# Issuing the V gather of a turn ahead of the U gather, in a hybrid mLSTM / attention / PEER encoder step

## What is computed

```
q = (xb @ w_q).reshape(TB, PEER_HEADS, PEER_KEY_DIM)
...
idx = jnp.take_along_axis(cidx, sel, axis=-1)
g = jax.nn.softmax(top.astype(jnp.float32), axis=-1).astype(xb.dtype)
u = jnp.take(expert_u, idx, axis=0)
a = jax.nn.gelu(jnp.einsum('thkd,td->thk', u, xb), approximate=False)
ve = jnp.take(expert_v, idx, axis=0)
return jnp.einsum('thk,thkd->td', g * a, ve)
```

## Time and profile before

| | before |
|---|---|
| median of 3 runs | 3383.86 us (3382.38 to 3389.47) |
| the profiled execution, its time | 3354.33 us |
| its span | 3352.6 us |
| VectorE busy | 2147.1 us (64%) |
| TensorE matmul busy | 2349.4 us (70%) |
| GpSimd busy | 1992.9 us (59%) |
| moved by DMA | 1197.59 MB, mean 357 GB/s |

### The profile page before, as it was taken

One profiled execution on the slowest core, in us unless ns is written; L12 is line 12 of the kernel. 1 busy time (PEld: TensorE's weight loads), 2 busy tenths in 40 slices (PEclk: granted clock), 3 DMA queues, 4 the chain that ended last, 5 costly groups with the idle time before them and its releaser, 6 DMA issues.

```text
span 3352.6 us, 42363 instructions
## 1 busy us (share of the span) xinstructions
PE 2349.4 (70%) x15147; PEld 1174.5 (35%) x15147; DVE 2147.1 (64%) x5579; ACT 535.9 (16%) x1059; POOL 1992.9 (59%) x2128
## 2 busy tenths in 40 slices
PE   8995775667667888877857765668567765675545
PEld 4652352335233533334534432325223431221111
DVE  1257757776676656657577667676676676766653
ACT  2211111211121221112121111111111111210001
POOL 0036666666666566665666666666666666666665
PEclk9996796678566988987867776678676875566555
DMA  6479999999999999999999999999999999999998
GB/s 229 149 277 405 358 349 375 362 373 349 375 357 381 368 402 408 408 400 357 362 353 365 366 369 363 360 372 351 376 361 374 364 353 377 359 359 362 368 368 325
DMA packets 348955, 1197.59 MB, mean 357 GB/s; under 512 B 37760, under 2 KB 54408, under 8 KB 346952
## 3 DMA queue, kind: packets, MB, share of 16 engines
q0 software_dynamic: 304128, 1107.43, 87.8%
q1 hardware_dynamic: 44616, 87.45, 7.1%
HBM read 1180.69 MB, written 14.15 MB: 356 GB/s over the span
## 4 chain that ended last, share of the span: by engine, by line
PE 31%; issue 16%; POOL 14%; DVE 13%; DMA 10%; another core or an unknown queue 9%; DVEq 5%; ACT 1%; ACTq 0%; SPq 0%; POOLq 0%
PE mx L1574 9%; PE acc L1675 7%; POOL ring L597 7%; POOL ring L586 7%; DVE ring L1273 6%; DMA ring<-in_peer_v_dram,idx 4%; PE mx L1385 3%; DMA ring<-in_peer_u_dram,idx 3%; DVEq L1145 2%; PE acc L1361 2%; PE mx L1585 2%; PE mx L1556 1%; DMA weights<-in_w_in_dram 1%; PE h2p L1628 1%
## 5 line engine op out<-in xcount | busy, mean ns | idle before, releaser
L1273 DVE SCALAR_TENSOR_TENSOR ring<-ring,h2p 128x1024 f32<-128x1024 f32 x1056 | 1272.2, 1214 | 551.7 <-DMA ring<-in_peer_u_dram,idx 267.5
L1675 PE MATMUL acc<-ring,wk 128*32 128x256 f32 x8448 | 1030.7, 507 | 684.6 <-DMA ring<-in_peer_v_dram,idx 317.5
L597 POOL DMA_INDIRECT ring<-in_peer_v_dram,idx x1056 | 995.3, 942 | 790.6 <-remote 369.4
L586 POOL DMA_INDIRECT ring<-in_peer_u_dram,idx x1056 | 995.8, 943 | 554.7 <-issue 302.4
L1675 PEld LDWEIGHTS acc<-ring,wk 128*32 128x32 f32 x8448 | 316.5, 129 | 1316.5 <-issue 776.9
L1574 PE MATMUL mx<-reg,weights 128*128 128x128 f32 x1792 | 275.3, 309 | 42.4 <-issue 42.1
L1574 PEld LDWEIGHTS mx<-reg,weights 128*128 128x128 f32 x1792 | 245.8, 216 | 101.5 <-issue 101.1
L1556 PE MATMUL mx<-weights,reg 128*128 128x512 f32 (+1 forms) x256 | 138.6, 668 | 1.9 <-DVEq L1246 1.1
L1385 PE MATMUL mx<-weights 128*128 128x512 f32 (+1 forms) x288 | 132.4, 604 | 2.2 <-issue 1.4
L1628 PE MATMUL h2p<-ch,ident 32*32 32x512 f32 x528 | 104.4, 798 | 31.2 <-issue 20.2
L828 ACT ACTIVATE gl<-dots 128x16 f32<-128x16 f32 x66 | 14.2, 216 | 537.8 <-issue 368.5
(11 more groups left out here) (311 smaller groups left out, 2425.6 us busy)
## 6 DMA issues: line engine op xcount, KB each, us to landing
ring<-in_peer_u_dram,idx POOLq DMA_INDIRECT x1056
ring<-in_peer_v_dram,idx POOLq DMA_INDIRECT x1056
weights<-in_peer_w_q_dram SPq DMA_DIRECT2D x7, 2048.0 KB
weights<-in_w_in_dram SPq DMA_DIRECT2D x5, 2048.0 KB, 18.2
weights<-in_w_in_dram SPq DMA_DIRECT2D x10, 1024.0 KB
ring<-in_peer_w_q_dram SPq DMA_DIRECT2D x8, 1024.0 KB, 6.1
xt<-in_x_prompt_dram SPq DMA_DIRECT2D x8, 512.0 KB
ring<-in_w_out_dram SPq DMA_DIRECT2D x2, 2048.0 KB, 13.6
```

Of the source, the lines that this page charges most:

```text
L586: pool.indirect_dma_start(ring[:, U_AT[n % NU], :], None, u_d, bass.IndirectOffsetOnAxis(ap=idx[:, g % 4, k:k + 1], axis=0)).then_inc(u_in ...
L597: pool.indirect_dma_start(ring[:, V_AT[n % NV], :], None, v_d, bass.IndirectOffsetOnAxis(ap=idx[:, g % 4, k:k + 1], axis=0)).then_inc(v_in ...
L1273: V.scalar_tensor_tensor(ring[:, U_AT[n % NU], :], ring[:, U_AT[n % NU], :], 1.0, h2p[:, :], ALU.mult, ALU.mult, accum_out=dots[:, (g + 1) ...
L1675: last = T.matmul(sums[g // 2 % 2][j * SUB:(j + 1) * SUB, :], wk[:, n // FEW % 5, n % FEW, :], ring[:, V_AT[n % NV], j * QD:(j + 1) * QD], ...
```

## The change

In a turn, the V gather of index n = 16 g + k is issued first and the U gather of index n + 16 behind it.

```diff
@@ -601,9 +601,9 @@
                 gather_u(0, k)
             for g in range(GROUPS):
                 for k in range(TOPK):
+                    gather_v(g, k)
                     if g + 1 < GROUPS:
                         gather_u(g + 1, k)
-                    gather_v(g, k)
 
 
         @block.scalar
```

## The result

The changed kernel takes 3392.2 us, the median of 20 runs (3383.5 to 3398.1), against 3384.05 us before, also of 20 runs: the ratio is 1.0020, with a 95% interval of 1.0012 to 1.0028. That is **8 us slower, where I forecast 27**. The sign was right and the size was not: the time lies under the 3395 to 3440 us that I had given for the forecast by itself.

The account below looks back on a forecast made before the run. The prediction saw a ring of several engines, each a little late for the next, none the bound by itself. Median 3384 us plus 27 us for late U gathers at group ends gave 3411 us; own range 3395 to 3440, full range 3353 to 3470.

Parts of the forecast that it names:

- GpSimd is held at V, not at U, and a held V gather keeps back U: GpSimd's queue: 328 holds at V gathers, almost none at U; each U gather behind one leaves 2.48 us later.
- The start costs nothing: First gathers: V gather 0 leaves some 12 us earlier, but the first V product waits for its weights; costed at nothing.
- Where VectorE was already waiting for U, the whole 2.48 us is passed on: 66 groups x 17.5% x 2.48 = 29 us: VectorE's last dot of each group: a U row one turn late costs the full turn where VectorE already waited; 29 us.
- lateness in the middle of a group is made good: VectorE's dots inside a group: it catches up before the group's end, so a late turn there was charged nothing.
- The second estimate, 11 U landings in the chain: Chain that ended last: left 11 times to a U landing, 11 x 2.48 = 27 us, the figure taken.
- transfers are the bound: DMA transfers from HBM: some 358 GB/s per core binds, order of issue moves nothing; 3384 us, chance 0.20 including catching up.
- TensorE gains more than VectorE loses: TensorE's V products: earlier V gathers save up to 1.7 us at each of 18 landings; 3353 us, chance 0.26.

Follow-up runs that it names:

- 6 and 8 buffers: 6 U and 8 V buffers in place of 7 and 7: ratio 1.0234 in the old order, 1.0100 with the V gather first, against the kernel before.
- half the bytes: Gathers fetch 512 floats in place of 1024: old order 0.9969 and 0.9968, new order 0.9956 and 0.9944, against the kernel before.
- Dot 1: Kernel before, with two extra VectorE multiplications by 1.0 ahead of the second dot behind `h2p` in every 32 dots: ratio 1.0031, 10 us slower.
- dot 31: Kernel before, with two extra VectorE multiplications by 1.0 ahead of the last dot of every second group: ratio 1.0020, 7 us slower.
- leads of 13: Kernel before, with 13 U gathers ahead of the V gathers in place of 17, for every first group of a pair 1.0141, for every second 1.0218.
- lead of 18: 18 U gathers ahead of V gather 0 in place of 17: ratio 1.0088; with 17 kept for indices 0 to 9 of 32: 1.0039.

## Why the prediction was right in sign and wrong in size

- **GpSimd is held at V, not at U, and a held V gather keeps back U**: right as a description of the waits. In both profiles of the change, V holds and VectorE's waits for U rose and TensorE's waits for V fell. With 6 and 8 buffers, where the holds at U have grown from 69 to 278 us, the same swap is a gain. But the sign of the time was in part luck: with half the bytes the same shift of waits went with a kernel that was 9 us faster.
- **The start costs nothing**: right; the first V products keep their time.
- **"Where VectorE was already waiting for U, the whole 2.48 us is passed on: 66 groups x 17.5% x 2.48 = 29 us"**: this is the step that failed, the term of the sum that was too large (27 us taken, 4 to 8 measured). The whole of a late turn is not passed on. Lateness put in by itself passed on 7 of 52 us ahead of a pair's last dot and 4 of 52 ahead of the other group's, a tenth of it in all. By the profiles of the two orders the rest is taken back from VectorE's waits for TensorE (`h2p`) and ScalarE (gelu), which mostly end when they did. The share was wrong as well, the other way: counted through the timeline, VectorE waited for U at 24 of the 66 last dots, 36% and not 17.5%, because its waits gather in the last four dots of a group (96 of 185). By the prediction's own rule that is 24 x 2.48 = 60 us, so the two errors partly cancelled. A tenth of 60 us is 6 us, which would fit the measured cost, but that is an estimate and no run shows that the cost is made up so.
- **"lateness in the middle of a group is made good"**, so charge only a group's end: wrong as a distinction. Dot 1 passes on a fifth, dot 31 an eighth. Delays of this size are mostly absorbed wherever they arise; leads of 13, which make one group in two late by four turns, cost 48 and 74 us.
- **The second estimate, 11 U landings in the chain**: it agreed with the first and was no confirmation. A second execution of the same kernel has 15 U and 15 V landings in its chain, where the first had 11 and 18, and the changed kernel has 18 and 16 in one execution and 16 and 18 in another. The count of landings in one chain therefore didn't price the change; that the pieces of several chains are nearly level here is my reading of it.
- **The rival "transfers are the bound"**: its time, 3384, was nearer than mine, but the half-byte kernels refute it as the bound of the whole: without half the gathered bytes the time falls by 0.3%. The part of it that named absorption was what happened, and that the order's cost vanishes with half the bytes says that the transfers bear on that cost. The rule in the Trainium skill, "DMA: Bandwidth & Descriptors", section Bandwidth, that for transfers between HBM and SBUF the HBM side binds at some 358 GB/s per core, doesn't set the time of this kernel: slices of it reach 402 to 411 GB/s, and at a mean of 191 GB/s in place of 357 it takes the same time within 0.3%.
- **TensorE gains more than VectorE loses**: not with 7 and 7 buffers, where TensorE gained 9 to 31 us in waits for V and VectorE lost 81 to 114 in waits for U. It did happen with 6 and 8 (55 gained, 34 lost).

What stays open: which resource fixes the level time of the ring. It is not the bytes and not VectorE's wait for U. What makes up the 4 to 8 us that the order does cost, and why they turn into a gain with half the bytes, is open too. Stops of GpSimd of 369 us are put down to `remote`, and no run took them apart. Why a lead of 18 still costs 13 us once more than half of the added holds at U are avoided isn't settled either.

## What to carry to other kernels

An in-order queue that feeds two rings makes the second stream wait whenever the first is held. Find out at which of the two it is held, from the waits of the issuing engine: the gather behind the held one is the one that comes late. Whether that costs time only a timed run says: here the same swap of order gave +0.2%, -1.3% with another split of the buffers, and -0.3% with half the bytes. And before the full length of a new wait is charged, look at how long the same engine waits right behind it for somebody else; a wait that grows in front of another wait mostly just moves, as long as the other is long enough, and the surest price is a run that inserts a known delay at that place.

## What was not expected of the hardware

A DMA busy share of nine tenths did not mean that the transfers were the limit. With half the bytes the gathers' queue still shows 57.0% of the 16 engines' time in place of 87.8%, not half of it. And the same kernel took 3384 us on one chip and 3360 on another, 0.7% apart, more than three times what the change is worth; only ratios on one chip could tell.
